# Products of a group accumulated in one PSUM bank, in the front stage of a pooling and attention trunk

## What is computed

```python
h = rms_norm(x, norm_g[l])
proj = jnp.einsum('bsd,de->bse', h, w_in[l])
u_pool, z_pool, q, k, v, z_attn, gate_logits = jnp.split(proj, splits, axis=-1)
y_pool = multiscale_pool(u_pool, pool_w[l], pool_scale[l]) * jax.nn.silu(z_pool)
attn = stick_breaking_attention(q.reshape(B, S, N_HEADS, HEAD_DIM),
                                k.reshape(B, S, N_HEADS, HEAD_DIM),
                                v.reshape(B, S, N_HEADS, HEAD_DIM))
y_attn = attn.reshape(B, S, ATTN_WIDTH) * jax.nn.silu(z_attn)
gates = jax.nn.sigmoid(gate_logits + b_gate[l]).reshape(B, S, 2, D)
merged = (gates[:, :, 0] * jnp.einsum('bsp,pd->bsd', y_pool, w_pool_up[l])
          + gates[:, :, 1] * jnp.einsum('bsa,ad->bsd', y_attn, w_attn_up[l]))
x = x + jnp.einsum('bsd,de->bse', merged, w_out[l])
return rms_norm(x, final_g)
```

## Time and profile before

| | us |
|---|---|
| runs | 1676.31, 1681.15, 1682.46 (median 1681.15) |
| profiled execution | 1675.41 |
| its span, first to last instruction | 1673.6 |
| TensorE busy in the span | 1558.0 (93%) |
| VectorE busy | 1332.8 (80%) |
| GpSimd busy | 1148.0 (69%) |
| ScalarE busy | 822.9 (49%) |
| granted TensorE clock, mean share of full speed | 0.973 |

### The profile page before, as it was taken

How to read it: one execution, slowest core, us unless ns; L and a number is a source line. 1 busy time by engine, 2 the same in 40 slices (tenths; PEclk the granted TensorE clock), 3 DMA queues, 4 the chain that set the end, 5 groups by cost and what they waited for, 6 DMA issues and landing times. The chain is left out here.

```text
span 1673.6 us, 25140 instructions
## 1 busy us (share of the span) xinstructions
PE 1558.0 (93%) x7770; PEld 1289.9 (77%) x7770; DVE 1332.8 (80%) x1753; ACT 822.9 (49%) x1601; POOL 1148.0 (69%) x802
## 2 busy tenths in 40 slices
PE   6898867999789999899999899999999999999998
PEld 4676656877578878788788788888888878887886
DVE  4768467796489888899789898889988865777987
ACT  4433334324256656566566566666666621233342
POOL 3675346765488877888788687878997534446774
PEclk9799888999999999999999999999999999999999
DMA  5346883136633423434359443342341488875453
GB/s 208 132 177 219 267 262 115 62 83 188 177 89 105 126 73 104 109 106 125 85 173 348 136 129 96 96 122 90 111 131 42 149 260 256 266 222 171 151 191 124
DMA packets 170277, 254.20 MB, mean 152 GB/s; under 512 B 48401, under 2 KB 81681, under 8 KB 170146
## 3 DMA queue, kind: packets, MB, share of 16 engines
q1 hardware_dynamic: 170146, 252.59, 48.7%
HBM read 166.54 MB, written 85.99 MB: 151 GB/s over the span
## 5 line engine op out<-in xcount | busy, mean ns | idle before, releaser
L1898 DVE TENSOR_TENSOR_SCAN left<-keep,left 128x512 f32<-128x512 f32 x192 | 301.4, 1570 | 39.1 <-issue 29.3
L1971 POOL TENSOR_TENSOR ring<-raw,ring 128x512 fp32r<-128x512 f32 x140 | 238.0, 1700 | 82.2 <-ACT ring L1805 67.0
L1725 PE MATMUL psum<-hT,ring 128*128 128x512 f32 x664 | 273.3, 412 | 9.3 <-ACT sum_a L1837 3.7
L1729 PE MATMUL psum<-hT,ring 128*128 128x512 f32 x664 | 271.4, 409 | 0.0
L1727 PE MATMUL psum<-hT,ring 128*128 128x512 f32 x664 | 271.2, 408 | 0.0
L1811 ACT ACTIVATE keep<-psum 128x512 f32<-128x512 f32 (+3 forms) x320 | 171.1, 535 | 130.2 <-PE psum L1748 113.6
L1818 ACT ACTIVATE wt<-psum 128x512 fp32r<-128x512 f32 (+3 forms) x320 | 171.1, 535 | 103.2 <-PE psum L1756 100.4
L1904 DVE TENSOR_TENSOR wt<-psum,wt 128x512 fp32r<-128x512 f32 (+3 forms) x320 | 189.6, 592 | 12.4 <-ACT wt L1818 9.4
L1768 PEld LDWEIGHTS psum<-wt,vm 128*128 128x128 f32 x1088 | 171.4, 189 | 34.0 <-DVE wt L1904 4.3
L1768 PE MATMUL psum<-wt,vm 128*128 128x256 f32 x1088 | 182.0, 282 | 6.6 <-DVE wt L1904 3.5
L747 POOL TENSOR_TENSOR ring<-raw,ring 128x512 fp32r<-128x512 f32 x76 | 110.2, 1451 | 112.0 <-ACT ring L908 105.9
(11 more groups left out here) (245 smaller groups left out, 3546.9 us busy)
## 6 DMA issues: line engine op xcount, KB each, us to landing
raw<-in_w_strips SPq DMA_DIRECT2D x144, 256.0 KB, 4.1
qm<-qk_scratch SPq DMA_DIRECT2D x128, 128.0 KB, 4.4
gate<-gate_scratch SPq DMA_DIRECT2D x64, 256.0 KB, 4.8
form_scratch<-hT SPq DMA_DIRECT2D x28, 512.0 KB, 6.8
hT<-form_scratch SPq DMA_DIRECT2D x28, 512.0 KB, 7.8
qk_scratch<-front_store SPq DMA_DIRECT2D x32, 256.0 KB, 4.0
km<-qk_scratch SPq DMA_DIRECT2D x64, 128.0 KB, 3.6
merged_scratch<-rows SPq DMA_DIRECT2D x32, 256.0 KB, 5.0
```

Of the source, the lines that this page charges most:

```text
L1725: pe.matmul(o, hi, m_hi, start=k == 0, stop=False)
L1729: last = pe.matmul(o, lo, m_hi, start=False, stop=k == HK - 1)
L1898: dve.tensor_tensor_scan(left[:, n % LN, span][:, ::-1], k, k, carry, ALU.mult, ALU.bypass).then_inc(scanned, 1)
L1971: pool.tensor_tensor(out_, a, b, op).then_inc(s, 1)
```

## The change

1. *Sums.* The partial sums of Strassen-Winograd are made on TensorE where products only add up. A11, S2, S3 and A22 of a group write one bank (0 or 3, by turns of groups) without clearing it, A12 writes bank 1, and S1 and S4 write bank 2. ScalarE copies the running content out three times (`take` of A11, S2 and S1, that is A11, A11+S2, and S1), and VectorE adds three times instead of seven (A12, S3, S4). The fourth result, A22, is complete in the bank: for u ScalarE copies it (`close_u`), for q and k the high part is copied and the low part subtracted straight from the bank. The part S2 now waits for the copy of A11, S3 for the copy of S2, S4 for that of S1, and A22 for the sum of S3.
2. *Result tiles.* `out_c` is a place of its own; A22 shares it with S3 and no longer `front_out_a` with A12.
3. *x places.* The first half's rows of x and transposed x get more places (`xt_ring`, `xT_more`), so their loads are issued earlier. The factors 1/rms are made in batches: tiles 0, 1, 2, 3, then 4 and 5, 6 and 7, then 8 to 15 at once. `pool_w` is loaded after the tiles and once more for the second half.
4. *Pooling.* One step a slot; the high part of its result is copied by ScalarE (`pooled_high`) instead of VectorE. The products stand after parts 14, 20, 25 and 29 of a half. The first group's weight forms on VectorE stand after the last tile's forms. The statistics of the second half start four parts earlier, the reload of v's weights two parts later, x of tiles 8 to 10 two parts earlier.

```diff
-FRONT_ADD = {A12: 1, S2: 2, S1: 3, S3: 4, S4: 6, A22: 7}
-OUT_TILE = {A12: 0, S4: 1, S3: 2, A22: 0}
+FRONT_ADD = {A12: 1, S3: 2, S4: 3}
+FRONT_TAKE = {A11: 1, S2: 2, S1: 3}
+OUT_TILE = {A12: 0, S4: 1, S3: 2, A22: 2}
...
-    def bank(r):
-        return psum[:, r % 4, :]
+    def bank(g, j):
+        return psum[:, 1 if j == A12 else 2 if j in (S1, S4) else g % 2 * 3, :]
...
+    OPENING = (A11, A12, S1)
...
+                slot = max(slot, part_slot(HALF_PARTS * f + FORMS * (q // 2) + (S4 if q % 2 == 0 else A22)) + 2)
+                for step in range(LEVELS[q] + 4):
+                    at_slot[f, q, step] = slot + step
+                slot += LEVELS[q] + 3
...
-    STAT_PARTS = {n: 14 + 2 * (n - FRONT_TILES) for n in range(FRONT_TILES, TT)}
-    RELOAD = 28
+    STAT_PARTS = {n: 10 + 2 * (n - FRONT_TILES) for n in range(FRONT_TILES, TT)}
+    BATCHES = ((0, 1), (1, 2), (2, 3), (3, 4), (4, 6), (6, 8), (8, 16))
+    RELOAD = 30
...
+            for n in (4, 5):
+                load_xt(n)
+                load_xT(n)
...
             def tile_step(n):
                 i = n % FRONT_TILES
-                if n < FRONT_TILES and later(n):
+                tile_high(n)
+                if batch_at(n) is not None:
                     square(n + 2)
-                tile_high(n)
-                if n < FRONT_TILES and later(n):
-                    root(n + 2)
+                    square(n + 3)
...
-            def take(g):
-                act.wait_ge(part_done, FORMS * g + A11 + 1)
-                if g:
-                    act.wait_ge(summed, 7 * g)
-                act.activation(sum_a, bank(FORMS * g + A11), ACT.Copy).then_inc(taken, 1)
+            def take(g, j):
+                act.wait_ge(part_done, FORMS * g + j + 1)
+                if j == S1:
+                    act.wait_ge(summed, 3 * g + FRONT_ADD[A12])
+                elif g:
+                    act.wait_ge(summed, 3 * (g - 1) + FRONT_ADD[S3 if j == A11 else S4])
+                act.activation(sum_u if j == S2 else sum_a, bank(g, j), ACT.Copy).then_inc(taken, 1)
...
+            def pooled_high(f, q):
+                act.wait_ge(level, levels_upto(f, q + 1))
+                if mix_use(f, q, 0):
+                    act.wait_ge(mixed, mix_use(f, q, 0))
+                act.activation(pl_hi[:, :], levels_of[LEVELS[q] % 2][:, PAD:W], ACT.Copy).then_inc(pool_hi, 1)
...
+                dve.wait_ge(taken, 3 * g + FRONT_TAKE[{A12: A11, S3: S1, S4: S2}[j]])
+                wait_tile_stored(dve, g, j)
+                dve.tensor_tensor(out_tile(g, j), bank(g, j), sum_u if j == S4 else sum_a, ALU.add).then_inc(summed, 1)
...
-                    if w % FORMS == A11:
+                    if w % FORMS == (A11 if w else None) or w == 2:
                         first_block_forms(w // FORMS)
...
-                if r >= 4:
-                    wait_bank(pe, r - 4)
...
+                if j == A11:
+                    if g >= 2:
+                        wait_closed(pe, g - 2)
...
+                elif j == A22:
+                    pe.wait_ge(summed, 3 * g + FRONT_ADD[S3])
+                else:
+                    pe.wait_ge(taken, 3 * g + FRONT_TAKE[{S2: A11, S3: S2, S4: S1}[j]])
...
+                                  k == 0 and j in OPENING, k == HK - 1, j not in OPENING)
```

More of the change, by code:

```diff
@@ L70, in __call__, with split3 @@
         return t
[L73 to L77, removed]
+def split3(pe, out, w_hi, w_lo, m_hi, m_lo, start, stop, onto=False):
+    pe.matmul(out, w_hi, m_hi, start=start, stop=False, skip_group_check=onto)
+    pe.matmul(out, w_hi, m_lo, start=False, stop=False, skip_group_check=onto)
+    return pe.matmul(out, w_lo, m_hi, start=False, stop=stop, skip_group_check=onto)
 def half(hT, block, k, part):
@@ L560, in step_at, with batch_of, batch_at @@
         return STEP_AT.get(s)
+    def batch_of(n):
+        return next(b for b, (first, end) in enumerate(BATCHES) if first <= n < end)
+    def batch_at(n):
+        return batch_of(n + 2) if n < FRONT_TILES and n % 2 == 0 and later(n) else None
     def later(n):
@@ L939, in _ @@
                     g, j = divmod(r, FORMS)
-                    if j == A11:
-                        take(g)
+                    if j in FRONT_TAKE:
+                        take(g, j)
+                    elif j == A22 and is_u(g):
+                        close_u(g)
                 n = step_at(s)
@@ L959, in _ @@
                     copy_v(n)
-                if s == 5:
-                    act.wait_ge(pool_in, 2 * DMA)
-                    act.activation(pw_hi[:, :, :], pw[:, :, :], ACT.Copy).then_inc(pw_hi_done, 1)
+                for f in range(2):
+                    if PART_AT.get(s) == HALF_PARTS * f + PW_PART + 3:
+                        mix_weights_high(f)
+                for f, q, step in pooling_at_slot(s):
+                    if step == LEVELS[q] + 1:
+                        pooled_high(f, q)
                 for f, q in mixes_at(s - 1):
@@ L969, in _ @@
                         square(n)
-                    if PART_AT.get(s - 2) == first:
-                        root(n)
-                if r is not None and RELOAD + 3 <= r < RELOAD + 3 + WV:
-                    weights_hi(1, r - RELOAD - 3)
+                        if n == TT - 1:
+                            root(batch_of(n))
+                if r is not None and RELOAD + 4 <= r < RELOAD + 4 + WV:
+                    weights_hi(1, r - RELOAD - 4)
                 if r == HALF_PARTS - 5:
@@ L1035, in tile_step @@
                 i = n % FRONT_TILES
-                first = n < FRONT_TILES and later(n)
-                if first:
-                    mean(n + 2)
                 scale(n)
-                if first:
-                    factors(n + 2)
                 if i % 2 == 1:
@@ L1167, in _ @@
             factors(3)
-            pools = [pooling(f) for f in range(2)]
-            nexts = [next(p) for p in pools]
             for s in range(SLOTS + 2):
```

345 lines of the change are left out of this document (191 added, 154 removed).

## The result

| | before | changed |
|---|---|---|
| runs, us | 1676.31, 1681.15, 1682.46 | 1635.84, 1637.44, 1638.69 |
| median | 1681.15 | 1637.44 |
| span of the profiled execution | 1673.6 | 1635.7 |
| TensorE / VectorE / ScalarE / GpSimd busy | 1558.0 / 1332.8 / 822.9 / 1148.0 | 1544.1 / 1280.3 / 845.6 / 1160.1 |

The ratio is 0.9746, 95% interval 0.9713 to 0.9779: 43.7 us faster. The forecast was 1646, with a range of 1614 to 1674.

The account below looks back on a forecast made before the run. The front stage before 458 us had 110 us that were not matmul work, with VectorE waiting 37.7 us for stores of `front_out_a`. Gains 20 + 5 + 1 + 6 = 32 from 1675.4 gave 1643.4, with an allowance 1646; range 1614 to 1674.

Parts of the forecast that it names:

- First tiles: Before part 2: weight forms end at 75, plus 16 of GpSimd low parts, part 2 at 91; 5 us gained (1 to 9).
- First half's parts: From 96.1 to 254 us: 157.9 become 137.6, with new losses of 15, 2 and 5; 20 us gained (5 to 35).
- the signs of being wrong: TensorE waiting on copies at all eight seams or S3 and S4; part 2 after 96; late stalls over 20 us.
- Removed sums: Four of seven VectorE sums a group and eight casts moved to ScalarE: 40 us costed at nothing directly.
- Low part's wait for S3's store: A22's low part waits for S3's store, delaying the sum behind it 0 to 3 us only when stores are slow.
- Pooling: Products 6, 5 and 4 parts apart give copy-out more slots; the 5.5 us wait behind the third goes, with 3 slow clock.
- last parts: Second half's parts: 5 us lost before 406 gone, 13 of 14 behind it kept; 6 us gained (12 gained to 6 lost).
- DMA: First half's parts: 16 engines busy 118 us, landings get later; 328 GB/s decides, hence 5 us kept per seam.
- Copies that cost nothing: Rival, chance 0.25: seams cost 0 to 2 us each as stores land in 4; 53 us gained, 1625.
- the gain given back: Rival, chance 0.08: late k, q, v loads stall the tail, first tiles gain nothing, seams cost 6.8; 9 gained, 1669.
- no effect: Rival, chance 0.05: VectorE's sums were hidden and the seams only change their name; 1681 us.
- the slower case: Rival, chance 0.07: A22's high part holds A11's copy at all eight seams, 6.8 us each; 7 slower, 1688.

Follow-up runs that it names:

- forms_first: The changed kernel with the first group's two weight forms on VectorE ahead of the last tile again; 1634.80 us, ratio 0.9744.
- three_halves: The changed kernel with a third place for the high parts on their way to HBM; 1632.16 us, ratio 0.9733.
- four_tiles: The changed kernel with a third place for the high parts and a fourth tile for A22's low part; 1626.51 us, ratio 0.9688.
- five_groups: The changed kernel with an idle VectorE pass at each of the four removed sums, in the first five groups of each half; 1639.80 us, ratio 0.9758.
- tiles_alone: The kernel before with only A22 moved to S3's tile, except in the first half's last group; 1670.56 us, ratio 0.9945.
- products_later: The kernel before with A22 in S3's tile and pooling products at parts 14, 20, 25 and 29 of a half; 1673.20 us, ratio 0.9972.
- all_room: The changed kernel with a third high-part place, a fourth tile for A22, x tile 11 moved and loaded earlier, first weight forms before the last tile; 1613.18 us.
- sums_back: The changed kernel with two idle VectorE additions beside each of the four removed sums a group; 1658.07 us, ratio 0.9889.

## Why the prediction was right, and where it was not

- **First tiles: 5 forecast, 9.4 measured; mis-sized.** The form "end of the weight forms plus 16" held in the change (in forms_first, where GpSimd has tile 7 in between, it was 17.9). The forms ended at 70.8 and not 75. The last weight form on VectorE, and GpSimd's next instruction:

```profile
70.10 0.69 DVE L1186 TENSOR_TENSOR front_second<-raw,raw 128x512 f32<-128x512 f32 x1
70.87 1.26 POOL L831 TENSOR_TENSOR raw<-front_second,raw 128x512 f32<-128x512 f32 x1 [6.64 <-DVE front_second L1186]
```

  and 70.8 + 16 is the 86.7 of part 2. I had added VectorE's durations from rows where GpSimd worked beside it (1.77 and 1.67); here GpSimd was idle for 6.64 us, and the two weight forms took 0.68 and 0.69, as did five of the last tile's six steps before them. That I took the move of these forms as free beside early x was a second miss: forms_first shows 4.2 us more to be had.
- **First half's parts: 20 forecast, 18.7 measured, in part by luck.** The new losses were forecast as 15 at three seams, 2 and 5. TensorE's starts in the changed kernel, in order of time, with the waits of the first seam (there is none at the second, and the third is the 8.64 above):

```profile
153.29 0.79 PE L75 MATMUL psum<-hT,ring 128*128 128x512 f32 x1 [4.67 <-ACT front_sum_a L979]
...
162.48 0.50 PE L75 MATMUL psum<-hT,ring 128*128 128x512 f32 x1 [2.10 <-ACT front_sum_u L979]
```

  That is 15.4 us of waits, and the window of 138.7 less the 115.6 of work loses 23.1, so 7.7 are slow clock and the start. The forecast's 15 had the slow clock in it. Counted by the starts that come later than 0.2267 us after the one before, the first seam lost 10.4 us and the third 11.2, 21.6 together against 15 forecast; the start lost 1.7 against 2, and the rest next to nothing against 5. Two misses of 5 to 7 us cancel. The mechanism stands, three_halves and four_tiles show it; its sizes were uneven, none at one seam and twice the 5 at the other two. S3 waited too, 2.10 and 0.81 us, which stood among the signs of being wrong: the copy of A11+S2 stands behind A12's high part as that of A11 stands behind A22's.
- **Removed sums: nothing directly, measured nothing** (five_groups, 27 of the 33 us). But "nothing directly" was not the whole of their worth: tiles_alone shows that the result tile, to which I gave the 27 us of the three waits, brings only 6.8 without them. The forecast summed the two edits as if each stood alone. The total holds only because both were made.
- **Low part's wait for S3's store: 0 to 3 us, "only when stores are slow".** 7.7 us in 3 waits, up to 5.3. In the change TensorE never stops for it by name, and it is the next bound as soon as `front_store` had room. What I named as late next was right, its size not.
- **Pooling: a step that failed.** The wait behind the third product did go, but not because its copy-out has slots more; products_later has those slots and keeps 11.0 us of such waits. They were ScalarE held at the seams, as the forecast's own first part had said of the longest. The placement itself brought 2.2 us in the first half and took more in the second.
- **Second tiles 1 and last parts 6: measured 1.4 and 6.4.** The end goes as described in the main: one seam lost 8.12 us there, with VectorE's wait for v up from 8.3 us to 11.6 (15.2 in two). That SP's order is the cause was not tested.

```profile
398.82 0.80 PE L75 MATMUL psum<-hT,ring 128*128 128x512 f32 x1 [8.12 <-ACT front_sum_a L979]
```

- **DMA.** "Above 260 GB/s" came out as 261. The 328 that I took as the trace's ceiling was an average over the whole stage; with the engines full the window of 28 us shows 359, and shorter stretches more. First in the change, then in all_room:

```profile
190.00:200.00 10.00, 9.88 (x44) 7.86 (x42) 1.99 (x3) 2.07 (x4) 2.90 (x3) 1.00 1.03 397
```

```profile
160.00:190.00 30.00, 30.00 (x134) 24.75 (x133) 15.21 (x18) 16.18 (x27) 17.61 (x13) 1.00 1.03 397
```

  The Trainium skill (DMA: Bandwidth & Descriptors, Specifications) gives about 358 GB/s as the HBM limit of a core. These rows do not agree with it as a ceiling: this core moved 397 for 30 us. By that figure the sum would have been 9 us lower, 1637, which meets the measured time by luck: the way there, loaded seams of 2 us, was wrong. Two of them took 6.8 and 8.6 us of waits, behind stores of S3 that landed 9.4 and 12.8 us after issue.
- **Rivals.** Copies that cost nothing (1625) fell by 24.3 us of waits on them; the gain given back (1669) and no effect by the mark; the slower case needed 6 us at all eight seams, and three had it (6.8, 8.6 and 8.1). The median of 1637.4 lies between the forecast and the first rival.
- **The total.** 32 us were forecast against 38.0 between the profiled executions: 4.4 of the difference are the first tiles, 1.9 lie behind the mark, where nothing was changed, and the other stages nearly cancel. The 2.8 us put on top for the runs' median were not needed; the changed kernel's profiled execution is its median.

## What to carry to other kernels

When an engine waits for a store before it can reuse a place, count the places along the whole chain (high part, low part, sum) and give room at each: with room for the high parts alone the wait moved and 3.5 us came, with room at both 16.4. Price edits on the same chain together: the tile alone was worth 6.8, the sums with the new places of the pooling 6.0, and all of them some 27. And before believing a run with added work, read what the added work took: here 94 us where 33 were meant.

## What was not expected of the hardware

- VectorE's additions from SBUF took 0.68 us with GpSimd idle and 1.67 to 1.78 with GpSimd at work beside them (the L1181 and L1186 rows of the change and of forms_first). An addition of 248 columns took 0.98 us in the mean in sums_back, longer than a pass over 512 columns of PSUM (0.686). The Trainium skill (SBUF — State Buffer, Who interferes with whom) has VectorE and GpSimd share a pair of ports, and a VectorE instruction with two SBUF inputs contend with a GpSimd instruction that reads SBUF; these rows agree.
- With DMA share 1.00 for 28 us the stores of `front_store` in the middle of it landed 12.8 to 13.0 us after issue, three times the 4.1 of the earlier trace rows. all_room moves 301 GB/s in the mean of the parts, with the engines full too from 160 to 190 us, and TensorE's longest wait on the copies is 3.5 us: in these kernels full DMA engines cost most where a place is missing.
